# Delta rule's silu, squares, gates and factors of q and k beside S5's end and its gate; the modulation's slabs behind them and in the inverse

## The reference

```python
mod = silu(c) @ w_ada + b_ada                     # six parts of 1024
y = gelu(y_scan + d_skip * u)                     # S5's output
y = y * sigmoid(y @ w_glu + b_glu)                # S5's gate
# delta rule
q, k, v = split(silu(causal_depthwise_conv(qkv, conv_w)))
q = q * rsqrt(sum(q * q) + EPS) * 128 ** -0.5;  k = k * rsqrt(sum(k * k) + EPS)
beta = sigmoid(b_gate);  g = -exp(a_log) * softplus(a_gate + dt_bias)
g = cumsum(g);  decay = exp(where(causal, g_i - g_j, -inf))
a_mat = where(strict, (k * beta) @ k.T * decay, 0) + eye
sol = triangular_solve(a_mat, [v * beta, k * beta * exp(g)])
# then a scan over chunks, rmsnorm and silu(z), concatenation with y, @ w_out
```

## Time and profile before

| | us |
|---|---|
| median of 3 runs | 2805.86 |
| lowest, highest | 2802.09, 2806.77 |
| the profiled execution | 2811.89 |
| its span | 2810.1 |
| granted TensorE clock over it (share of 2.4 GHz) | 0.98 |
| S5's last product ends, in the trace | 201.6 |
| inverse begins, ends | 279.0, about 316 |

### The profile page before, as it was taken

One profiled execution on the slowest core, in us unless ns is written; L12 is line 12 of the kernel. 1 busy time (PEld: TensorE's weight loads), 2 busy tenths in 40 slices (PEclk: granted clock), 3 DMA queues, 4 the chain that ended last, 5 costly groups with the idle time before them and its releaser, 6 DMA issues.

```text
span 2810.1 us, 36376 instructions
## 1 busy us (share of the span) xinstructions
PE 2710.2 (96%) x15082; PEld 2326.5 (83%) x15082; DVE 1748.8 (62%) x1957; ACT 1249.0 (44%) x1588; POOL 136.8 (5%) x227
## 2 busy tenths in 40 slices
PE   7988989999999999999999999999999999999998
PEld 6977878888878897888889888888978888897887
DVE  6883467767656637565666666666455666655665
ACT  3202246656444446444444444445454444445443
POOL 4000000000000001001000000000000010000000
PEclk9998989999999999999999999999999999999999
DMA  7431147878655454656544655654535556453652
GB/s 254 159 111 62 59 164 263 304 280 302 210 187 192 159 174 148 205 187 203 187 165 150 235 196 178 200 180 143 173 120 181 197 175 212 165 168 118 217 180 90
DMA packets 349489, 509.42 MB, mean 181 GB/s; under 512 B 14880, under 2 KB 295488, under 8 KB 349328
## 3 DMA queue, kind: packets, MB, share of 16 engines
q1 hardware_dynamic: 342960, 484.17, 51.2%
q0 software_dynamic: 5792, 20.78, 2.2%
q10 hardware_dynamic: 576, 2.20, 0.2%
HBM read 506.04 MB, written 1.05 MB: 180 GB/s over the span
## 4 chain that ended last, share of the span: by engine, by line
PE 87%; DVE 7%; ACT 2%; DMA 2%; issue 1%; POOL 0%; SPq 0%; DVEq 0%; POOLq 0%; ACTq 0%
PE psum L425 18%; PE psum L426 18%; PE psum L427 18%; PE psum L805 15%; PE psum L806 8%; PE psum L1237 2%; PE psum L2407 1%; PE psum L2406 1%; DVE raw_r L412 1%; PE psum L2419 1%; PE psum L2438 1%; PE psum L1598 1%; DMA arena<-in_w_up 0%; PE psum L819 0%; DMA wlo_f<-in_w_up 0%
## 5 line engine op out<-in xcount | busy, mean ns | idle before, releaser
L412 DVE TENSOR_TENSOR raw_r<-raw,whi 128x2048 fp32r<-128x2048 f32 x185 | 421.7, 2290 | 163.9 <-ACT whi L404 163.2
L404 ACT ACTIVATE whi<-raw 128x2048 fp32r<-128x2048 f32 x185 | 350.5, 1906 | 11.1 <-DMA raw<-in_w_up 8.5
L412 DVE TENSOR_TENSOR place_lo<-arena,place_hi 128x2048 fp32r<-128x2048 f32 x107 | 244.2, 2290 | 94.9 <-ACT place_hi L404 94.9
L806 PE MATMUL psum<-act_both,place_lo 128*128 128x256 f32 x944 | 264.1, 280 | 0.0
L893 ACT ACTIVATE scratch<-scratch 128x256 f32<-128x256 f32 x112 | 46.8, 418 | 462.7 <-DVE scratch L969 462.7
L805 PE MATMUL psum<-act_both,place_hi 128*128 128x512 f32 x704 | 247.9, 392 | 0.0
L805 PE MATMUL psum<-act_both,whi 128*128 128x512 f32 x640 | 228.5, 398 | 0.0
L404 ACT ACTIVATE place_hi<-arena 128x2048 fp32r<-128x2048 f32 x107 | 202.5, 1904 | 2.1 <-DMA arena<-in_ff_w_in 2.0
L425 PE MATMUL psum<-whi,act_both 128*128 128x256 f32 (+1 forms) x552 | 180.2, 326 | 5.4 <-DVE act_both L661 3.2
L806 PEld LDWEIGHTS psum<-act_both,place_lo 128*128 128x128 f32 x944 | 177.8, 188 | 2.4
L806 PE MATMUL psum<-act_both,raw_r 128*128 128x256 f32 x640 | 179.6, 281 | 0.0
(11 more groups left out here) (556 smaller groups left out, 6587.8 us busy)
## 6 DMA issues: line engine op xcount, KB each, us to landing
arena<-in_ff_w_in SPq DMA_DIRECT2D x182, 512.0 KB, 5.1
raw<-in_ff_w_in SPq DMA_DIRECT2D x126, 512.0 KB, 4.9
arena<-in_ff_w_out SPq DMA_DIRECT2D x88, 512.0 KB, 4.6
raw<-in_ff_w_out SPq DMA_DIRECT2D x68, 512.0 KB, 4.5
wlo_f<-in_ff_w_in SPq DMA_DIRECT2D x44, 512.0 KB, 4.9
raw<-in_w_ada SPq DMA_DIRECT2D x20, 1024.0 KB, 5.2
raw<-in_w_gate SPq DMA_DIRECT2D x35, 512.0 KB, 4.2
raw<-in_w_up SPq DMA_DIRECT2D x35, 512.0 KB, 5.9
```

The costliest lines, as they stand in the source:

```text
L404: act.activation(hi, loaded, ACT.Copy).then_inc(S("slab_hi"), 1)
L412: dve.tensor_tensor(lo, loaded, hi.bitcast(F32), ALU.subtract).then_inc(S("slab_lo"), 1)
L806: last = pe.matmul(both[:, 0, :], lo[:, c, g, cs], act_hi[:, k, :], start=False, stop=k == KD - 1)
```

## The change

ACT's silu, squares, root and gate functions move from `gdn_act` into `s5_act`: silu and squares ahead of gelu, the root, the exponentials and the logarithm behind S5's split and ahead of the gate's sigmoid, for whose table a small warm-up is added. The squares get another place in the arena. On DVE the gates' steps and the diagonals move from `gdn_dve` into `s5_dve`, around the split's low half and ahead of the gate's multiplication. On PE the column sums take the place of slab 8 behind S5's products, the rows of the factors follow the gate's products directly, and slabs 8 to 11 stand where 11, 12, 14 and 15 stood. Slabs 12 to 15 go into levels 1 to 4 of the inverse, between P and Q; DVE reads each at its level's end. PSUM banks are exchanged accordingly. No product, function or load is added but the warm-up of one column; line numbers behind L1403 shift.

The diff, cut to its core (what `gdn_act` and `gdn_dve` lose is what `s5_act` and `s5_dve` gain):

```diff
--- before.py
+++ after.py
@@ -1402,6 +1402,8 @@
         k_t = area(4, 1024).rearrange("p (c t) -> p c t", c=HEADS)
         v_t = scratch[:, 1024:2048].rearrange("p (c t) -> p c t", c=HEADS)
         qkv = [q_t, k_t, v_t]
+        sq = arena[:, 12 * 1024:14 * 1024]
+        qk_r, o_r = tiny(16), tiny(8)
         PADT = T + CONV - 1
         pads = [scratch[:, 2048 + s * 2 * PADT:2048 + (s + 1) * 2 * PADT].rearrange("p (m t) -> p m t", m=2) for s in range(2)]
         ab_bank = psum[:, 7, 0:16].rearrange("p (t e) -> p t e", t=NT)
@@ -1500,14 +1502,14 @@
                     pe.matmul(y, cx_nim[:, j, :], q3[:, m, :], start=False, stop=False)
                     last = pe.matmul(y, cx_nim[:, j, :], q4[:, m, :], start=False, stop=True)
                 last.then_inc(S("s5_y"), 1)
-            ada_pe(pe, ADA_FIRST + 8)
+            pe.wait_ge(S("qk_sq"), 2)
+            column_sums(pe, psum[:, 2, 0:16], sq, S("head_sums"))
 
             pe.wait_ge(S("glu_lo"), 2)
             pe.wait_ge(lo_ready[GD], PLAN.base["w_glu"][GD] + 1)
             for m in range(2):
                 last = proj_t(pe, slab_views(GD, 4), m, act_k=CS5, m0=2 * m)
             last.then_inc(slab_used[GD], 1)
-            ada_pe(pe, ADA_FIRST + 9)
 
         def s5_dve(dve, done):
             dve.wait_ge(S("s5_pool"), S5_POOL["table"][6])
@@ -1551,23 +1553,55 @@
             dve.wait_ge(S("s5_y"), 8)
             for m in range(CS5):
                 dve.scalar_tensor_tensor(act_f[:, m, :], u[:, m, :], col("s5_d", m), s5_y(m), ALU.mult, ALU.add).then_inc(S("s5_yd"), 1)
-            ada_dve(dve, done, ADA_FIRST + 8)
+            dve.wait_ge(S("gates_raw"), 1)
+            a_v = psum[:, 7, 0:16].rearrange("p (t e) -> p e t", t=NT)
+            heads_v = [ap.rearrange("p (h t) -> p h t", h=HEADS) for ap in (g_s, bg_s)]
+            done(dve.tensor_tensor(heads_v[0], a_v[:, 0:4, :], col("dt_bias", 0, TH).rearrange("p (h t) -> p h t", h=HEADS), ALU.add))
+            done(dve.tensor_copy(heads_v[1], a_v[:, 4:8, :]))
+            done(dve.tensor_scalar(e_s, g_s, -1.0, None, ALU.mult))
+            done(dve.tensor_scalar(sp_s, g_s, 0.0, None, ALU.max))
+            dve.tensor_tensor(e_s, e_s, g_s, ALU.max).then_inc(S("gate_in"), 1)
             for q in range(2):
                 dve.wait_ge(S("glu_hi"), q + 1)
                 dve.tensor_tensor(act_lo[:, 2 * q:2 * q + 2, :], act_f[:, 2 * q:2 * q + 2, :],
                                   act_hi[:, 2 * q:2 * q + 2, :].bitcast(F32), ALU.subtract).then_inc(S("glu_lo"), 1)
+            dve.wait_ge(S("head_root"), 1)
+            done(dve.reciprocal(qk_r, qk_r))
+            diagonals(dve, qk_diag, qk_r, S("head_diag"))
+            dve.wait_ge(S("gdn_act"), GDN_ACT["gate_exp"][2])
+            done(dve.tensor_scalar(bg_s, bg_s, 1.0, None, ALU.add))
+            done(dve.reciprocal(beta_s, bg_s))
+            dve.wait_ge(S("gdn_act"), GDN_ACT["gate_ln"][0])
+            done(dve.tensor_tensor(sp_s, sp_s, e_s, ALU.add))
+            done(dve.scalar_tensor_tensor(g_s, sp_s, -1.0, ea_s, ALU.mult, ALU.mult))
+            dve.tensor_copy(th_view(g_b), bc(g_s, P)).then_inc(S("g_rows"), 1)
+            dve.tensor_copy(th_view(beta_b), bc(beta_s, P)).then_inc(S("g_rows"), 1)
             sg = arena[:, 14336:15360].rearrange("p (m t) -> p m t", m=CS5)
             for m in range(CS5):
                 dve.wait_ge(S("glu_gate"), m + 1)
                 dve.tensor_tensor(act_f[:, m, :], act_f[:, m, :], sg[:, m, :], ALU.mult).then_inc(S("act_f"), 1)
-            ada_dve(dve, done, ADA_FIRST + 9)
 
         def s5_act(act):
+            for i in range(3):
+                act.wait_ge(S("convolved"), 2 * i + 2)
+                act.activation(qkv[i], qkv[i], ACT.Silu).then_inc(S("qkv"), 1)
+            for i in range(2):
+                act.wait_ge(S("qkv"), i + 1)
+                act.activation(sq[:, i * 1024:(i + 1) * 1024], area(3 + i, 1024), ACT.Square).then_inc(S("qk_sq"), 1)
             for q in range(2):
                 act.wait_ge(S("s5_yd"), 2 * q + 2)
                 act.activation(act_f[:, 2 * q:2 * q + 2, :], act_f[:, 2 * q:2 * q + 2, :], ACT.Gelu_apprx_tanh).then_inc(S("glu_f"), 1)
                 act.wait_ge(S("glu_f"), q + 1)
                 act.activation(act_hi[:, 2 * q:2 * q + 2, :], act_f[:, 2 * q:2 * q + 2, :], ACT.Copy).then_inc(S("glu_hi"), 1)
+            act.wait_ge(S("head_sums"), 1)
+            act.activation(qk_r, psum[:, 2, 0:16], ACT.Sqrt, bias=eps_col).then_inc(S("head_root"), 1)
+            act.wait_ge(S("gate_in"), 1)
+            act.activation(e_s, e_s, ACT.Exp, scale=-1.0).then_inc(S("gdn_act"), 1)
+            act.activation(bg_s, bg_s, ACT.Exp, scale=-1.0).then_inc(S("gdn_act"), 1)
+            act.activation(ea_s, col("a_log", 0, TH), ACT.Exp).then_inc(S("gdn_act"), 1)
+            act.wait_ge(S("gdn_act"), GDN_ACT["gate_exp"][0])
+            act.activation(e_s, e_s, ACT.Ln, bias=one_col).then_inc(S("gdn_act"), 1)
+            act.activation(warm, warm, ACT.Sigmoid)
             sg = arena[:, 14336:15360].rearrange("p (m t) -> p m t", m=CS5)
             act.wait_ge(slab_used[GD], PLAN.base["w_glu"][GD] + 1)
             for m in range(CS5):
@@ -1605,8 +1639,7 @@
         def tok_view(ap):
             return ap.rearrange("p (c t) -> p c t", t=T)
 
-        sq, qk_diag = arena[:, 6 * 1024:8 * 1024], arena[:, 8 * 1024:10 * 1024]
-        qk_r, o_r = tiny(16), tiny(8)
+        qk_diag = arena[:, 8 * 1024:10 * 1024]
         g_b, beta_b, kb_t, eg = blk(10), blk(11), blk(12), blk(13)
         diff = blk(6)
         n_t, qk_t = blk(7), blk(8)
@@ -1627,48 +1660,44 @@
             v = ap.rearrange("p (b two n) -> p b two n", two=2, n=1 << lv)
             return v[:, :, odd, :]
 
+        INV_ADA = {1: ADA_FIRST + 12, 2: ADA_FIRST + 13, 3: ADA_FIRST + 14, 4: ADA_FIRST + 15}
+
         def gdn_pe(pe):
             upto = mat("upto")
 
-            pe.wait_ge(S("qk_sq"), 2)
-
-            pe.wait_ge(S("glu_gate"), CS5)
-            column_sums(pe, psum[:, 0, 0:16], sq, S("head_sums"))
-            ada_pe(pe, ADA_FIRST + 10)
-
+            rows_of(pe, 2, qk_diag, S("head_diag"), 0, S("head_rows"))
             pe.wait_ge(S("g_rows"), 2)
             pe.matmul(psum[:, 7, 32:32 + TH], upto, g_s, start=True, stop=True).then_inc(S("gdn_pe"), 1)
+            pe.wait_ge(S("glu_gate"), CS5)
             for e in range(TH):
-                last = pe.matmul(banks(4)[:, e * P:(e + 1) * P], th_view(g_b)[:, e, :], upto, start=True, stop=True)
+                last = pe.matmul(banks(0)[:, e * P:(e + 1) * P], th_view(g_b)[:, e, :], upto, start=True, stop=True)
             last.then_inc(S("gdn_pe"), 1)
-            ada_pe(pe, ADA_FIRST + 11)
-            rows_of(pe, 0, qk_diag, S("head_diag"), 0, S("head_rows"))
+            ada_pe(pe, ADA_FIRST + 8)
 
             pe.wait_ge(S("qk_normed"), 2)
             for e in range(TH):
-                last = pe.matmul(banks(0)[:, e * P:(e + 1) * P], th_view(beta_b)[:, e, :], ident, start=True, stop=True)
+                last = pe.matmul(banks(2)[:, e * P:(e + 1) * P], th_view(beta_b)[:, e, :], ident, start=True, stop=True)
             last.then_inc(S("gdn_pe"), 1)
-            ada_pe(pe, ADA_FIRST + 12)
+            ada_pe(pe, ADA_FIRST + 9)
 
             pe.wait_ge(S("kb"), 1)
             pe.wait_ge(S("diff"), 1)
+            pe.wait_ge(S("gdn_act"), GDN_ACT["eg"][0])
             kn, qn, kb = (tok_view(b) for b in (blk(4), blk(3), kb_t))
-            for bank, rhs in ((2, kb), (4, qn)):
+            for bank, rhs in ((4, kb), (0, qn)):
                 for e in range(TH):
                     ts = slice((e % 2) * P, (e % 2 + 1) * P)
                     last = pe.matmul(banks(bank)[:, e * P:(e + 1) * P], kn[:, e // 2, ts], rhs[:, e // 2, ts], start=True, stop=True)
                 last.then_inc(S("gdn_pe"), 1)
-            ada_pe(pe, ADA_FIRST + 13)
-
             for e in range(TH):
-                last = pe.transpose(banks(0)[:, e * P:(e + 1) * P], blk(4)[:, e * P:(e + 1) * P], ident)
+                last = pe.transpose(banks(2)[:, e * P:(e + 1) * P], blk(4)[:, e * P:(e + 1) * P], ident)
             last.then_inc(S("gdn_pe"), 1)
-            ada_pe(pe, ADA_FIRST + 14)
+            ada_pe(pe, ADA_FIRST + 10)
             pe.wait_ge(S("n_qk"), 2)
             for e in range(TH):
-                last = pe.transpose(banks(2)[:, e * P:(e + 1) * P], scratch[:, 1024 + e * P:1024 + (e + 1) * P], ident)
+                last = pe.transpose(banks(4)[:, e * P:(e + 1) * P], scratch[:, 1024 + e * P:1024 + (e + 1) * P], ident)
             last.then_inc(S("gdn_pe"), 1)
-            ada_pe(pe, ADA_FIRST + 15)
+            ada_pe(pe, ADA_FIRST + 11)
 
 
             pe.wait_ge(S("nat_read"), 1)
@@ -1685,6 +1714,8 @@
                         else:
                             last = pe.transpose(p_at, n3[:, e, :], ident)
                     last.then_inc(S("inv_p"), 1)
+                if lv in INV_ADA:
+                    ada_pe(pe, INV_ADA[lv])
```

(56 more changed lines are left out.)

13 lines of the change are left out of this document (removed).

## The result

The changed kernel takes 2784.35 us (median of 5 runs, 2779.93 to 2788.62) against 2806.77 before (5 runs, 2802.09 to 2810.37): ratio 0.9925, 95% interval 0.9908 to 0.9943, 22.4 us faster. The forecast was 2782 and its range 2776 to 2794. On two other occasions, each beside its own runs of before, it took 2788.20 against 2806.06 (0.993, 0.9916 to 0.9944) and 2785.19 against 2802.53 (0.9928, 0.9914 to 0.9942): 17.9 and 17.3 us.

What follows compares the result with a forecast made beforehand. PE bounds the kernel, busy 96% of the span, so only its idle time and low clock can pay: 12.7 + 10.9 = 23.6 us off the 2805.9 median, 2782 us, range 2776 to 2794.

Steps and rivals of the forecast that it cites:

- PE's idle time: From S5's end to the inverse, five PE stops of 14.1 us go, less 1.4 us of new waiting: 12.7 us gained.
- New stops: Waiting of 1.4 us: 0.6 ahead of the gate's products, 0.45 at the inverse's first mask, 0.35 at level 5's.
- The clock's term: Column sums, slab 10, rows of the factors, beta's rows and products of k run at full clock: 10.9 us gained.
- signs of being wrong: PE idle over 2 us at named steps, clock 0.50 behind 212 us, late sigmoid, or w_out's second split after the inverse.
- The price of a low stretch: PE's half-clock time on steps around its stops was counted as recoverable, 1.55 to 3.15 us per step.
- Slabs in the inverse: Slabs 12 to 15 in levels 1 to 4 cost 3.45 us each, as before the inverse: no gain, no loss.
- Rival 1: Column sums hold the clock down through gate and half the rows of the factors: gain 16 us, 2790; chance 0.10.
- The 1.7 us that a full clock in the gate was to give: Forecast's own bound: no low clock in the gate's products would give 1.7 us more.
- Rival 2: PE waits for DVE, diff only 0.2 us ahead; two 2.4 us stops remain: gain 16 us, 2790; chance 0.10.
- Rival 3: PE gets 1.2 GHz in the inverse, 49 us of full-clock work costing 49 more: 2831, slower; chance 0.03.
- w_out's slabs: Behind the inverse, ACT splits both w_out slabs some 4 us before DVE wants them.
- Table loads: ACT's four loads take 1.28 us each, sigmoid ready at 211.5; at the skill's 2.66 us, PE would wait about 1.5.

Runs made afterwards that it cites:

- e7: The changed kernel with the gates' exponentials, logarithm and DVE steps moved back behind the sigmoid, its warm-up dropped: 2785.84 us against 2802.33 before (0.9945).
- e2: The kernel before with only silu of q, k, v and both squares moved ahead of gelu: 2794.99 us against 2802.33 before (0.9969).
- e9: The kernel before with four of its five stops filled by unused identity products, not the one ahead of the gate: 2798.97 us against 2802.53 (0.999).
- e1: The changed kernel run again, unedited: 2788.20 us against 2806.06 before.
- e12: The changed kernel run once more, unedited, for a third profile: 2785.19 us against 2802.53 before.
- e3: The changed kernel with slabs 12 to 15 in a row ahead of the inverse, none in its levels: 2783.56 us.
- e6: The kernel with slabs in levels 0 to 3, slab 8 put between column sums and gate, others one place up: 2782.60 us against 2778.70 without that.
- e10: The kernel with slabs in levels 0 to 3, its column sums taken with 128 columns of ones instead of one: 2778.82 us against 2779.58 without that.
- e5: The changed kernel with DVE reading slab 11 behind level 0's masks instead of ahead of them: 2786.34 us.

## Why the prediction was right, point by point

- *PE's idle time is the first term.* Right: 12.7 us forecast, 13.1 in the two traces. Column sums 3.73 us at full clock (3.7), the gate's start at 205.65 (205.9), rows of the factors at 212.98 (213.2), products of k at 227.18 (227.6), level 0 at 239.48 (239.8). No stop between the gate and the inverse.
- *New stops, 1.4 us.* The 0.6 ahead of the gate and the later first mask came (0.61, and 0.83 instead of 0.35). The 0.35 at level 5 didn't: slab 15's addition runs 283.15 to 283.56 and the mask starts at 283.49, before it is needed.
- *The clock's term, 10.9 us.* This is the mis-sized one. Per step the forecast held up to level 0 (beta's rows 1.79 us by the next row's start, products of k 3.64). But I had written that PE keeps 1.00 from there, since the inverse did, and had counted level 0's later mask as 0.45 us of waiting alone. A low stretch came there as well, and it cost 3.1 us (by the next row's start P 2.97 and slab 12 5.74, against 2.14 and 3.51 in e7). The traces leave 8.2 us for the clock. A clock of 0.50 behind 212 us was one of the prediction's own signs of being wrong, and the inverse ends at 294.4 instead of near 292. What is tied to the later mask isn't shown: e7 has the same mask and the same stops and kept its clock.
- *The price of a low stretch.* I took every stop of 2.3 to 2.5 us to cost a low stretch, because in the one profile of before each did. e2 kept four such stops and paid for two, e9 kept one and paid for none. That is probably why the medians of the three comparisons (22.4, 17.9, 17.3 us) lie below the 26.2 us between the two profiled executions, and below the 23.6 forecast. It is in part luck that the first comparison came within 2.4 us of 2782: I had taken the low stretches of one long execution off a median that may hold fewer of them, and beside e1 and e12 the same sum misses the gain by some 6 us.
- *Slabs in the inverse cost their 3.45 us and gain nothing.* Right, by e3.
- *Rival 1 (the sums hold the clock down)* was right in its mechanism and small in its place: they let it fall in the changed kernel for 3.4 us of the gate, as I had counted, and for over 6.6 us in e6 and in e2. The 1.7 us that a full clock in the gate was to give were 1.5: its products take 5.86 us in e10 (203.51 to 209.37) for 7.33.
- *Rival 2 (DVE late)* didn't occur: diff was there at 227.07, PE came at 227.18. The slack was 0.1 us. e7 shows what a late DVE costs, though ahead of g's rows and not of the products of k: 3.37 us of stop and a low stretch.
- *Rival 3* named the right thing, a lower clock in the inverse, with a size far too large: 49 us of work at half clock, where 3.1 us were lost.
- *w_out's slabs* were ready in time: ACT's second split ended at 288.9, DVE wanted it at 294.2.
- *Table loads.* 1.28 us each with the next operation at once (204.89 to 206.19 to 206.48), so the sigmoid was warm at 211.3 and PE didn't wait. The drain that the Trainium skill adds (page ScalarE: Activation LUTs, section What ACT_TABLE_LOAD costs) is not seen here.

Left open: why the clock stayed up at level 0 in e7 with the same stops, why it fell behind the inverse in e5 and e10, and how often the kernel before pays for its stops; one profile of it can't tell. So of the whole gain the 13.1 us of idle time are firm (the stops that e2 leaves as they were came again at 2.27, 2.52, 2.44 and 2.53 us), and the clock's share is known for the profiled executions only.

## What to carry to other kernels

Fill PE's stops with work that exists anyway, taken from where it covers nothing: the same four slabs were worth nothing in levels 1 to 4 and 4.4 us of stretch when the first covered level 0, 3.55 of them also when all four stood in a row ahead of it. Judge such a change by the stretch between two fixed events, which repeated within 0.03 us here while whole runs spread over nearly 9; but look in it for low stretches at places that the change doesn't touch, as e9's gate, where 1.5 us went by chance. And when one profile of a kernel shows a low clock behind every stop, take that as the upper bound of what it costs, not as its price.

## What the runs showed that I had not expected

- Behind one-column products the clock fell with PE busy throughout: e6, no stop around them, 0.50 from 204 to 210.6 us. The same 32 records with 128 columns took 3.84 instead of 3.73 us, and the clock stayed at 1.00.
- Stops of 0.83 and 0.54 us with transposes between them were followed by some 6.8 us at 0.50 in three profiles of three of the changed kernel and by none in e7, while in e2 two of three stops of 2.5 us were followed by none. The length of a stop alone doesn't say what it costs.
- A low stretch removed at one place came up at another (e10, at 286 us), which gave back the 1.5 us gained in the gate.
